# Attention output turned back by four plain turns, with VectorE adding the two parts, in place of products with a two-block unit table

## The reference

```python
    def query_block(i):
        ...
        s = (jnp.einsum('bqgrd,bgqkd->bgrqk', qb, kg)
             - slopes[None, :, :, None, None] * dist.astype(f32))
        p = jax.nn.softmax(jnp.where(dist >= 0, s, NEG_INF), axis=-1)
        o_sel = jnp.einsum('bgrqk,bgqkd->bqgrd', p, vg)
        ...
        pw = jax.nn.softmax(jnp.where(mw, sw, NEG_INF), axis=-1)
        o_win = jnp.einsum('bgrqk,bkgd->bqgrd', pw, vwb)
        return o_sel, o_win
    ...
    gate = jax.nn.sigmoid((gate_logits + gate_b).astype(f32)).reshape(B, S, G, R, N_NSA_BRANCH)
    o = gate[..., 0:1] * o_cmp + gate[..., 1:2] * o_sel + gate[..., 2:3] * o_win
```

## Time and profile before

| | |
|---|---|
| median of 3 runs | 4210.89 us (4206.26 to 4212.6) |
| the profiled execution's own time | 4219.19 us |
| its span | 4217.2 us |
| mean granted TensorE clock, as a share of full speed | 0.952 |
| TensorE busy | 3839.8 us, 91% of the span |
| VectorE busy | 2457.9 us, 58% |
| ScalarE busy | 1996.7 us, 47% |
| GpSimd busy | 578.8 us, 14% |

### The profile page before, as it was taken

How to read it: one execution, slowest core, us unless ns; L and a number is a source line. 1 busy time by engine, 2 the same in 40 slices (tenths; PEclk the granted TensorE clock), 3 DMA queues, 4 the chain that set the end, 5 groups by cost and what they waited for, 6 DMA issues and landing times. The chain is left out here.

```text
span 4217.2 us, 69303 instructions
## 1 busy us (share of the span) xinstructions
PE 3839.8 (91%) x26480; PEld 3139.9 (74%) x26481; DVE 2457.9 (58%) x4173; ACT 1996.7 (47%) x3165; POOL 578.8 (14%) x945
## 2 busy tenths in 40 slices
PE   7999999999988878999888877999599999999798
PEld 5777877777767646777777766999478888888687
DVE  2545555555556427777777655444576555567565
ACT  2434433344333216666666653222276555567565
POOL 1111111111121112112212210000110000001120
PEclk9999999999999978999999988999699999999899
DMA  4534434443333350000000006433388666689642
GB/s 129 152 99 111 134 107 111 123 118 92 106 98 88 78 123 23 14 13 19 16 19 19 21 13 190 133 124 105 150 332 325 235 237 228 226 318 363 252 149 94
DMA packets 512853, 557.18 MB, mean 132 GB/s; under 512 B 106188, under 2 KB 374476, under 8 KB 511532
## 3 DMA queue, kind: packets, MB, share of 16 engines
q1 hardware_dynamic: 479988, 461.10, 34.7%
q0 software_dynamic: 16416, 59.78, 3.8%
q10 hardware_dynamic: 16176, 32.55, 2.1%
HBM read 439.78 MB, written 113.57 MB: 131 GB/s over the span
## 5 line engine op out<-in xcount | busy, mean ns | idle before, releaser
L555 PE MATMUL fr_fb<-fr_hT_h,fr_w_h 128*128 128x512 f32 (+1 forms) x1312 | 536.1, 409 | 11.0 <-ACT fr_zs L836 7.6
L555 PE MATMUL fr_fb<-fr_hT_r,fr_w_h 128*128 128x512 f32 (+1 forms) x1312 | 531.9, 405 | 0.0
L555 PE MATMUL fr_fb<-fr_hT_h,fr_w_r 128*128 128x512 f32 (+1 forms) x1312 | 531.6, 405 | 0.0
L1005 DVE TENSOR_TENSOR fr_w_r<-fr_w_raw,fr_w_h 128x1024 fp32r<-128x1024 f32 (+1 forms) x164 | 197.9, 1207 | 498.4 <-ACT fr_w_h L809 497.4
L2065 DVE TENSOR_TENSOR aq_p_lo<-aq_t_bank,aq_p_hi 128x512 fp32r<-128x512 f32 x412 | 283.0, 689 | 192.1 <-ACT aq_p_hi L1958 184.8
L1958 ACT CAST aq_p_hi<-aq_t_bank 128x512 fp32r<-128x512 f32 x412 | 238.5, 581 | 249.7 <-PE aq_t_bank L1865 244.0
L836 ACT COPY fr_zs<-fr_fb 128x512 f32<-128x512 f32 (+1 forms) x148 | 87.0, 588 | 509.2 <-PE fr_fb L555 508.7
L555 PEld LDWEIGHTS fr_fb<-fr_hT_h,fr_w_h 128*128 128x128 f32 (+1 forms) x1312 | 248.8, 190 | 79.1 <-ACT fr_zs L836 13.2
L555 PEld LDWEIGHTS fr_fb<-fr_hT_h,fr_w_r 128*128 128x128 f32 (+1 forms) x1312 | 249.0, 190 | 63.4 <-issue 11.1
L555 PEld LDWEIGHTS fr_fb<-fr_hT_r,fr_w_h 128*128 128x128 f32 (+1 forms) x1312 | 249.1, 190 | 62.2 <-issue 10.9
L134 PE MATMUL ex_gu<-wx_gate_w,ex_xT 128*128 128x512 f32 x1176 | 288.5, 401 | 3.6 <-DVE ex_xT L2848 3.6
(11 more groups left out here) (495 smaller groups left out, 8672.0 us busy)
## 6 DMA issues: line engine op xcount, KB each, us to landing
wk_raw<-in_w_exp_gate_up SPq DMA_DIRECT2D x64, 2048.0 KB, 10.9
fr_w_raw<-in_w_in SPq DMA_DIRECT2D x160, 512.0 KB, 3.9
wk_raw<-in_w_exp_down SPq DMA_DIRECT2D x32, 2048.0 KB, 10.1
s_z<-fr_zs SPq DMA_DIRECT2D x160, 256.0 KB
s_rows<-ex_y ACTq DMA_DIRECT2D x50, 512.0 KB, 4.3
mx_mg<-s_z SPq DMA_DIRECT2D x32, 512.0 KB, 7.3
fr_zc<-s_z SPq DMA_DIRECT2D x15, 903.0 KB, 6.8
sh_shared<-in_x SPq DMA_DIRECT2D x16, 512.0 KB, 5.2
```

The costliest lines, as they stand in the source:

```text
L555: ins = pe.matmul(bank[0:cols_, :], (w_h, w_h, w_r)[p][:, k, c, 0:cols_].bitcast(F32R), (hT_h, hT_r, hT_h)[p][:, c, :].bitcast(F32R), star ...
L1005: dve.tensor_tensor(w_r[:, m % 2, :, 0:cols_].bitcast(F32R), w_raw[:, m % 2, :, 0:cols_], w_h[:, m % 2, :, 0:cols_], ALU.subtract).then_in ...
```

## The change

The product with `pair` becomes a plain turn of each head's 128x128 tile with the unit matrix `ident`, which leaves both parts in `misc`, 512 columns in place of 256. VectorE adds them by one `tensor_reduce` that reads pairs 64 columns apart in `misc` and writes 256 columns into the first half of `oT`. It gives `misc` free right after that, and then scales by one instruction with the four scales spread out, into `y` where it is the first to write, or in place and followed by one addition to `y`. Since `oT` is now used by VectorE too, ScalarE's next `take_out` waits for the whole combine (`y_ok`) and no longer for the turning alone. The table `pair` and the three instructions that build it are gone.

```diff
--- before.py
+++ after.py
@@ -1466,7 +1466,7 @@
         qf = take(QF * R * P).rearrange("p (k h t) -> p k h t", k=QF, h=R)
         t_cmp, keep_t, force_t = take(256), take(64), take(64)
         t_win, rows_ok = kp.sb("t_win", [P, WK]), kp.sb("rows_ok", [P, 1])
-        overlap, pair = kp.sb("overlap", [P, N_SEL]), kp.sb("pair", [P, HD])
+        overlap = kp.sb("overlap", [P, N_SEL])
         q_raw = kp.sb("q_raw", [P, G, R, P])
         q_s = kp.sb("q_s", [P, 2, G, R, P])
         q_in, q_high, q_ok = (kp.lasting_sem(n, Z["whole"]) for n in ("q_in", "q_high", "q_ok"))
@@ -1589,9 +1589,6 @@
                 masked(overlap[:, :], [[-4, N_SEL]], 1, 1, 0.0)
                 masked(overlap[:, :], [[4, N_SEL]], 2, -1, 0.5)
                 masked(overlap[:, :], [[4, N_SEL]], 3, -1, 0.0)
-                step(pool.memset(pair[:, :], 0.0))
-                for d in range(2):
-                    masked(pair[:, :], [[-1, HD]], -d * HD, 1, 1.0, ALU.not_equal)
                 split_q(pool, 0)
                 split_q(pool, 1)
 
@@ -1845,7 +1842,7 @@
                         pe.wait_ge(ot_ok, F.at[t, k // 2, k % 2] + 1)
                         misc_free(n)
                         for h in range(R):
-                            ins = pe.matmul(misc[:, h * HD:(h + 1) * HD], oT[:, h, :], pair[:, :], start=True, stop=True)
+                            ins = pe.transpose(misc[:, h * P:(h + 1) * P], oT[:, h, :], ident[:, :])
                     if kind == "turn_y":
                         pe.wait_ge(y_ok, F.at[t, G - 1, SEL] + 1)
                         misc_free(n)
@@ -1940,8 +1937,7 @@
                 def take_out(n, u):
                     act.wait_ge(pv_made, n - 1)
                     if u:
-                        t, g, b = F.units[u - 1]
-                        act.wait_ge(misc_made, F.misc["back", t, 2 * g + b] + 1)
+                        act.wait_ge(y_ok, u)
                     act.copy(flat(oT[:, :, :]), o_bank[:, :]).then_inc(ot_ok, 1)
 
                 for n in STEPS:
@@ -2019,16 +2015,20 @@
                     v.link(dve.reciprocal(weight[:, :], total[:, u % UR, :]))
                     v.link(dve.tensor_tensor(weight[:, :], weight[:, :], gate, ALU.mult))
                     dve.wait_ge(misc_made, n + 1)
+                    parts = misc[:, :].rearrange("p (h k d) -> p h d k", h=R, k=2)
+                    room = flat(oT[:, :, :])[:, 0:R * HD].rearrange("p (h d) -> p h d", h=R)
+                    v.link(dve.tensor_reduce(room, parts, AX.X, ALU.add))
+                    dve.sem_inc(misc_read, 1)
+                    scales = weight[:, :].rearrange("p (h o) -> p h o", o=1).to_broadcast([P, R, HD])
                     if b == WIN and not F.out_is_first(t, g):
-                        ins = dve.tensor_tensor(y[:, t % Y, g, :, :], misc[:, 0:R * HD].rearrange("p (h d) -> p h d", h=R),
-                                                weight[:, :].rearrange("p (h o) -> p h o", o=1).to_broadcast([P, R, HD]), ALU.mult)
+                        ins = dve.tensor_tensor(y[:, t % Y, g, :, :], room, scales, ALU.mult)
                     else:
                         if F.out_is_first(t, g):
                             dve.wait_ge(misc_read, F.misc["out", t, g] + 1)
-                        ins = add_scaled(t, g, lambda h: weight[:, h:h + 1])
+                        v.link(dve.tensor_tensor(room, room, scales, ALU.mult))
+                        ins = dve.tensor_tensor(y[:, t % Y, g, :, :], y[:, t % Y, g, :, :], room, ALU.add)
                     ins.then_inc(y_ok, 1)
                     dve.wait_ge(y_ok, u + 1)
-                    dve.sem_inc(misc_read, 1)
 
                 def event(kind, t, k):
                     n = F.misc.get((kind, t, k))
```

## The result

The changed kernel takes 4260.2 us (median of 4 runs, 4256.2 to 4267.0) against 4209.4 for the kernel before on the same chip (4 runs, 4206.3 to 4212.6): a ratio of 1.0122, 95% interval 1.0105 to 1.0140, so 51 us more (44 to 59). The profiled executions differ by less, 4257.8 against 4219.2, since that of before lay 10 us above this median; what follows from the two traces has to add up to 39 us.

The account below looks back on a forecast made before the run. A ring of TensorE, VectorE and ScalarE waiting for each other was taken to bound the attention stage. 12.0 + 6.5 + 10.5 + 2.3 = 31 us on a median of 4210.9 gave 4242 us; range for 8 in 10, 4207 to 4268.

Parts of the forecast that it names:

- second rival: Saving and additions cancel: with the short reduction the path terms make about 19 us; 4211 to 4218 us, chance 0.14.
- signs of being wrong: TensorE's gaps not growing, a short reduction, unchanged waits for `p_lo`, or the stage's granted clock moving by more than 0.01.
- TensorE's part: Turning a unit back falls from 0.81 to 0.35 us, 0.46 cheaper; over 64 units at most 29.4 us.
- VectorE's addition: Reduction at 1.01 us (low bound 0.69): 1.09 more at 43 adding units, 1.06 at 21 others; 69 us in all.
- (a): Ahead of "turn_y": TensorE waits for a query block's last combine 11 times, each 1.09 us later: 12.0 us (short reduction: 8.5).
- (b): Combine followed by a mask, then an exponential: 6 waits for the odd buffer, each 1.09 us later: 6.5 us (short: 4.6).
- (c): At the 21 WIN units a later `p_lo` holds TensorE up 0.5 us on average: 10.5 us (short reduction: 4).
- (d): At the stage's last units ScalarE's copy to `oT` waits for VectorE's longer combine: 2.3 us after savings.
- `misc`: The bank comes free 1.01 us after the combine's start instead of 0.86; 8 "out" waits change by at most 0.2 each.
- GpSimd's table: Its three instructions cost nothing and removing them brings nothing: behind them GpSimd waits 20.54 us for the queries.
- The lower end of the forecast's own range: 4220 us, for a short reduction and half of (c); the forecast's own range, 4220 to 4262, has a chance of 0.55.
- The clock: Rival: the stage's mean granted clock falls from 0.93 to 0.90, 28 us more, giving 4270 us; chance 0.07.

Follow-up runs that it names:

- e1_turns_alone: The kernel before with four plain turns for the unit-table products, VectorE's instructions as before, second part of the values left out: ratio 0.9993, 3 us less.
- e2_sum_alone: The kernel before keeping the table product (entries 0.5), with VectorE adding the result to itself in the longer chain and ScalarE's late copy: ratio 1.0143, 60 us more.
- e4_queries_later: The changed kernel with GpSimd's split of a tile's queries starting only behind an addition: ratio 1.0099, 42 us above before, 9 below the change.
- e5_before_queries_later: The kernel before with GpSimd's split of a tile's queries starting only behind an addition of the tile two ahead: ratio 0.9995.
- e10_change_weights_early: The changed kernel with a unit's two 128x4 weight instructions made ahead of the addition, in place: ratio 1.0083, 35 us above before, 16 below the change.
- e6_late_release: The changed kernel with the turn bank given free only behind the whole addition: ratio 1.0151, 64 us above before, 12 above the change.
- e8_weights_early: The kernel before with a unit's two 128x4 weight instructions made ahead of the addition, in place in the sums: 4197.5 us, ratio 0.9962, 16 us less.

## Why the prediction was right, and where its sum was not

The sign and the mechanism were right: VectorE's longer addition lies on the path, TensorE's saving brings next to nothing, and the 31 us forecast came out as 51, inside the range. That it came so near is in part luck. The reduction was priced at 1.01 us and takes 0.69; by the prediction's own terms the sum is then about 19 us (its second rival names that figure), and two of its own signs of being wrong came true: the reduction is short, and the granted clock of the stage moved by more than 0.01. What filled the gap is mostly a fall of the clock that the sum left out, and some 10 us of stretching beside GpSimd that no term had.

- **TensorE's part**: the size was right (0.81 us down to 0.36), its worth too: 3 us alone, about 9 in the change, of 29.
- **VectorE's addition** was forecast at 69 us and the additions grew by 65.1 in sum (45.8 to 110.9), but not for the reasons given. The reduction took the low bound, 0.69; the row chosen, 1007 ns, was nearest in kind and wrong here. The gap behind the reduction was 0.15, not 0.04, for the release issued in it, 7 us in all. So an adding unit costs 1.72 (0.86 more) and a window unit 1.27 (0.85 more): 43 x 0.86 + 21 x 0.85 = 55 us. The other 10 are multiplications and additions stretched beside GpSimd (26.6 + 20.3 us against 86 x 0.425 = 36.6), a term that the prediction lacked. The Trainium skill, "SBUF — State Buffer", section "Who interferes with whom", states that a VectorE instruction with two SBUF inputs contends with GpSimd's reads of SBUF; the rows at 1988 agree (1.68 us beside GpSimd, 0.43 without), and it was a rule to be weighed when the change swapped reads of PSUM for reads of SBUF.
- **(a)** 12.0 forecast, the waits of the turned `y` grew by 11.5. The price of 1.09 was too high (0.86 as measured, 9.5 us for 11 places), and the cheaper turning alone lengthens these waits by 4.2 (`e1_turns_alone`), VectorE's half alone by 6.1 (`e2_sum_alone`: 20.3).
- **(b)** 6.5 forecast, the waits for the odd score buffer grew by 7.5. Not by a like amount each: the growth lies between 0.4 and 2.7 us, most behind stretched additions, and in `e4_queries_later` the row is at 12.8, a growth of 3.0. A first turn that waits for the even buffer, which the prediction didn't count, went from 1.65 to 5.35 us behind an addition of 4.27.
- **(c)** 10.5 us forecast for the 21 window units. TensorE's waits for `p_lo` grew by 23.3, but not all there. In the changed kernel 13 of these waits, 12.4 us in all, end within 2.2 us after VectorE has finished a unit that writes `y` itself, where the kernel before has none; so (c) came out about right. The waits that end as closely behind an adding unit grew by 5.1, and all others by 5.6: these are the places which the prediction set at nothing. The reason, "most of which falls into its idle time", held only in part: VectorE's idle time is mostly waiting for ScalarE within the ring (184.8 us in the earlier trace rows). And TensorE's own saving makes part of this growth, as the same row shows in `e1_turns_alone` and in `e2_sum_alone` (8.1 and 14.3 us more than the kernel before):

```profile
PE aq_t_bank L1865 <- DVE aq_p_lo L2065: 24.5, 40, 3.5
...
PE aq_t_bank L1865 <- DVE aq_p_lo L2068: 30.7, 46, 3.6
```

- **(d)** 2.3 us forecast for the last units in all. Over the last 12 `p_lo` copies the changed kernel's delay grows by 3.7 us; the late copy alone costs 6 (1 to 11) in the kernel before.
- **`misc`** neither gained nor lost, as forecast, since it is given free right behind the reduction: its wait went from 9.3 to 9.5. Had it been kept, 12 us more.
- **GpSimd's table** cost nothing, as forecast: the first `p_lo` copy of the stage comes 0.2 us later.
- **The lower end of the forecast's own range**, 4220, does not follow from its terms: 4211 + 19, less 2 for half of (c), is 4228.
- **The clock** is the term that was sized worst. It was priced as a rival with a chance of 0.07 and happened in part. Windows from the same first to the same last instructions, for the kernel before, `e5_before_queries_later`, `e1_turns_alone` and the changed kernel:

```profile
1590.00:2539.20 949.20, 817.44 (x4837) 685.41 (x4838) 686.56 (x1972) 594.82 (x1336) 192.12 (x190) 0.93 0.06 16
1596.40:2534.50 938.10, 804.67 (x4837) 675.00 (x4838) 683.94 (x1972) 595.13 (x1336) 192.26 (x190) 0.94 0.06 17
1583.80:2525.70 941.90, 793.41 (x4581) 654.21 (x4582) 684.65 (x1972) 594.88 (x1337) 192.15 (x190) 0.92 0.06 17
1590.00:2581.60 991.60, 803.94 (x4582) 662.06 (x4583) 737.49 (x1950) 595.18 (x1337) 192.25 (x190) 0.91 0.06 16
```

The first two kernels have the same TensorE instructions and, in the runs, the same time; that the traced execution of before is some 10 us above its median shows here as 13 us more of TensorE's own work at a lower clock. Against the second row, which lies within 2 us of its median, the change has 54 us more of gaps and TensorE busy less by only 0.7. The forecast had implied 60 us of gaps (31 + 29) and 29 less of busy time. So in sum the gaps came out near the forecast, and what it missed is TensorE's saving, which did not show as less busy time but went with the lower level: 10.5 us of it between the third row and the fourth, with the same instructions. With the levels at 1.2 and 2.4 GHz a mean of 0.94 is about 110 us of the stage at the lower one, 0.91 some 180 (the means are rounded, so 10 us either way). In the runs too the mean over the whole kernel is lower, 0.948 to 0.951 in the four of the change against 0.950 to 0.960, median 0.954, in those of before. It isn't the plain turns: `e2_sum_alone` has none of the new ones and 0.90, `e1_turns_alone` has all and 0.92. That longer gaps bring the lower level is argued only. The kernels with the VectorE work of before have 0.92 to 0.94 and those with more of it 0.89 to 0.91, but no run changed one without the other, and `e10_change_weights_early` gained 16 us with the clock still low. What decides it stays open.

The dose says most directly what the sum of all this is: one more us of addition, spread over all 64, costs about 1.2, gaps and clock together.

## What to carry to other kernels

Where three engines hand one tile round a ring, an engine's idle share can say little about the price of more work on it (here 1.2 us for each added us, with VectorE idle for a quarter of the stage): move work off the hand-over first (two 128x4 instructions a unit moved ahead brought 16 us), and put a dose on each engine before trading one's time for another's. Look at more than one execution before reading a few us out of a pair of traces: the clock alone moved TensorE's busy time by 13 us between two kernels of the same time. When an intermediate goes from PSUM to SBUF, look for GpSimd's long instructions beside it. And when work is added behind a shared bank, copy the bank out first and free it: that was worth 12 us here (2 to 22).

## What the runs showed of the hardware

- A `tensor_reduce` of pairs 64 elements apart in PSUM, 512 in and 256 out, takes 692 ns, as a contiguous `tensor_tensor` of 512 does (689); the one over SBUF, 16 apart and with 16 out, takes 1007.
- A dependent `tensor_tensor` starts 0.03 to 0.04 us after the end of such a reduction (`e6_late_release`), as after another `tensor_tensor`. With one semaphore increment issued between the two it starts 0.15 us after it (the changed kernel).
- A VectorE `tensor_tensor` of 128x256 with its inputs in SBUF, 0.43 us alone, takes 1.68 us when a GpSimd `tensor_tensor` of 2.37 us is under way, and ends 0.28 us behind it; a reduction that reads PSUM beside the same instruction keeps its 0.69.
- The same TensorE instructions of the stage took 806, 818 and 843 us in three kernels (`e8_weights_early`, before, `e2_sum_alone`) at granted clocks of 0.94, 0.93 and 0.90. The first two do not stand for the kernels: `e5_before_queries_later`, in the time of the kernel before, took 805 at 0.94.
